# The second block's second mixer: a new order for its projections, its stick-breaking groups and its memory attention

## The reference, cut to the stage in question

```python
h = rms_norm_2(x, norm_pre_mix[1])
proj = h @ w_in_b[0]                 # 256 tokens x 1024 -> 2560
q, k, v = three parts of 768, as 12 heads of 64
mem_q = proj[..., 2304:]             # 256 wide, 4 heads of 64
# stick-breaking attention, for each block of 128 queries and all keys up to its end
z = q @ k.T / 8
before = s_idx < t_idx
log_1m_beta = where(before, log_sigmoid(-z), 0)
tail = cumsum(log_1m_beta, reversed) - log_1m_beta
mix = where(before, exp(log_sigmoid(z) + tail), 0) @ v
# memory attention over 256 memory tokens, whose keys and values were made early on
cross = softmax(mem_q @ mem_k.T / 8) @ mem_v
y = concatenate([mix, cross]) @ w_out[1]
```

## Time and profile before

| what | value |
|---|---|
| runs | 2134.07 us median of 3 (2133.82 to 2136.89) |
| profiled execution | 2134.89 us, of which the span is 2132.7 us |
| mean granted TensorE clock | 0.979 |
| busy in the span | PE 2046.2 us (96%), DVE 1528.1 (72%), ACT 1247.1 (58%), POOL 21.6 (1%) |
| the chain that ended last | PE 85%, DVE 7%, ACT 4%, issue 3%, SP's queue 1% |
| HBM | 447.62 MB read, 210 GB/s over the span |

### The profile page before, as it was taken

The page is one execution under the profiler, slowest core; times in us unless marked ns, Lnnn a source line. Parts: engine busy times, 40 slices in busy tenths (PEclk is TensorE's granted clock), DMA queues, the critical chain, the costliest instruction groups (busy, mean ns, idle before and its releaser), DMA issues.

```text
span 2132.7 us, 31892 instructions
## 1 busy us (share of the span) xinstructions
PE 2046.2 (96%) x12731; PEld 1834.2 (86%) x12731; DVE 1528.1 (72%) x1741; ACT 1247.1 (58%) x1458; POOL 21.6 (1%) x52
## 2 busy tenths in 40 slices
PE   8989999988999999999999999899999999989998
PEld 8978998988787888888888888799999998878997
DVE  7866777575889888888888888676746556456554
ACT  5674434554767777676767777546255445655443
POOL 2000000000000000000000000000000000000000
PEclk9999999999999999999999999799999999999999
DMA  7314555432789898989898989333014554414552
GB/s 245 116 43 138 180 200 191 152 108 80 281 309 379 313 384 308 382 309 374 317 372 320 373 320 335 119 119 119 21 60 158 186 184 132 150 40 149 194 181 100
DMA packets 263790, 450.12 MB, mean 211 GB/s; under 512 B 10401, under 2 KB 147082, under 8 KB 263690
## 3 DMA queue, kind: packets, MB, share of 16 engines
q1 hardware_dynamic: 263304, 448.37, 60.0%
q10 hardware_dynamic: 386, 0.32, 0.0%
HBM read 447.62 MB, written 1.05 MB: 210 GB/s over the span
## 4 chain that ended last, share of the span: by engine, by line
PE 85%; DVE 7%; ACT 4%; issue 3%; SPq 1%; DMA 0%; ACTq 0%; DVEq 0%
PE bank L2329 23%; PE bank L2331 22%; PE bank L2330 22%; PE bank L2502 3%; PE bank L2455 2%; PE bank L2504 2%; DVE w_lo L1497 1%; DVE w_lo L1902 1%; ACT w_hi L918 1%; PE bank L2704 1%; PE bank L2861 1%; PE bank L2357 1%; PE bank L2426 1%; ACT w_hi L1201 1%; PE bank L2558 1%
## 5 line engine op out<-in xcount | busy, mean ns | idle before, releaser
L1497 DVE TENSOR_TENSOR w_lo<-ring,w_hi 128x2048 fp32r<-128x2048 f32 x160 | 365.4, 2291 | 205.5 <-ACT w_hi L918 205.2
L2329 PE MATMUL bank<-w_hi,a_both 128*128 128x512 f32 (+1 forms) x1040 | 372.6, 358 | 11.4 <-DVE a_both L1932 4.2
L2329 PE MATMUL bank<-a_both,w_hi 128*128 128x256 f32 x1248 | 359.5, 288 | 12.7 <-DVE a_both L1529 4.7
L918 ACT ACTIVATE w_hi<-ring 128x2048 fp32r<-128x2048 f32 x160 | 304.6, 1908 | 107.2 <-PE bank L2331 100.6
L2331 PE MATMUL bank<-w_hi,a_both 128*128 128x512 f32 (+1 forms) x1040 | 364.4, 350 | 0.0
L2330 PE MATMUL bank<-w_lo,a_both 128*128 128x512 f32 (+1 forms) x1040 | 363.9, 350 | 0.0
L1902 DVE TENSOR_TENSOR w_lo<-ring,w_hi 128x2048 fp32r<-128x2048 f32 x144 | 326.9, 2288 | 51.1 <-ACT w_hi L1201 51.1
L2330 PE MATMUL bank<-a_both,w_hi 128*128 128x256 f32 x1248 | 355.8, 285 | 0.0
L2331 PE MATMUL bank<-a_both,w_lo 128*128 128x256 f32 x1248 | 355.6, 285 | 0.0
L1201 ACT ACTIVATE w_hi<-ring 128x2048 fp32r<-128x2048 f32 x144 | 275.7, 1919 | 90.1 <-PE bank L2331 89.4
L1902 DVE TENSOR_TENSOR w_lo<-work,w_hi 128x2048 fp32r<-128x2048 f32 x120 | 274.7, 2289 | 19.2 <-ACT w_hi L1201 17.0
(11 more groups left out here) (440 smaller groups left out, 2855.4 us busy)
## 6 DMA issues: line engine op xcount, KB each, us to landing
ring<-in_moe_w_up SPq DMA_DIRECT2D x72, 1024.0 KB, 6.5
work<-in_moe_w_gate SPq DMA_DIRECT2D x72, 1024.0 KB, 7.2
ring<-in_moe_w_down SPq DMA_DIRECT2D x56, 1024.0 KB, 6.3
work<-in_moe_w_down SPq DMA_DIRECT2D x32, 1024.0 KB, 6.4
ring<-in_w_up SPq DMA_DIRECT2D x32, 1024.0 KB, 5.3
ring<-in_w_down SPq DMA_DIRECT2D x32, 1024.0 KB, 4.9
ring<-in_moe_w_gate SPq DMA_DIRECT2D x16, 1024.0 KB, 5.1
work<-in_moe_w_up SPq DMA_DIRECT2D x16, 1024.0 KB, 7.7
```

Source lines behind the costliest of these rows:

```text
L918: return eng.activation(w_hi[:, slot, :], ring[:, slot, :], ACT.Copy)
L1497: V.tensor_tensor(w_lo[:, i % SLOTS, :], ring[:, i % SLOTS, :], w_hi[:, i % SLOTS, :].bitcast(F32), ALU.subtract).then_inc(lo_made, 1)
L2329: PE.matmul(out, left[0], right[0], start=start, stop=False, **kw)
```

## The change

It reorders the stage and splits tiles into halves; the same matmuls are made. On TensorE:

- The tile of memory queries comes first (`T_MQ1`), with the norm's sums.
- Queries and keys follow by halves, `query_key(i)`, i = 0 to 11; the tiles alternate between queries and keys, so that tile 2k and 2k+1 give head pairs 2k and 2k+1. Scores of group g are made as soon as its pairs are there.
- Memory steps 0 to 12, score groups 0 to 3, sums and outputs stand between the halves of queries, keys and values, in an order written out by hand. The banks' numbers are given out in the same order.
- The first tile of the second output projection goes by chunks of the input, in the order 0, 1, 2, 6, 7, 3, 4, 5 (6 and 7 are the memory heads), each when its heads are there, instead of waiting for all.

On ScalarE, the softplus of a group, its exponential, value copies, high parts and memory steps follow in the matching order. The memory heads are copied out of their bank to `mem_heads` (in `h`) when a pair is done, and split from there later. On VectorE, the four scalings of memory queries come first; the rest is interleaved too. `feed_lo` of output tiles 1 and 2 stands behind the heads 0 and 1 and the memory heads and ahead of heads 2 to 5.

The diff, cut to its core:

```diff
+        Y1_ORDER = (0, 1, 2, 6, 7, 3, 4, 5)
+        mem_heads = h[:, 0:2, :]
...
         A_DN0 = lend(4)
+        A_O3 = lend(2)
         A_SB = lend(6)
-        A_O3 = lend(2)
         A_DN1 = lend(4)
-        H_O1, H_O2, H_SB, H_O3 = 0, 8, 10, 16
+        H_O1, H_O2 = 0, 8
+        H_O3, H_SB = (10, 14), (11, 12, 13, 15, 16, 17)
...
-        T_INB = stream(*[C(a["w_in_b_2"][0], t, U_INB_QK + 2 * t + 2) for t in range(6)])
-        stream(*[C(a["w_in_b_2"][0], 6 + t, V_USES[t] + 2) for t in range(3)])
-        stream((*column_tile(a["w_in_b_2"][0], 3 * SW), "done", U_MQ1 + 2))
+        T_MQ1 = stream((*column_tile(a["w_in_b_2"][0], 3 * SW), "done", U_MQ1 + 2))
+        T_QK = stream(*[C(a["w_in_b_2"][0], t // 2 + 3 * (t % 2), U_QK[2 * t + 1] + 1) for t in range(6)])
+        T_SV = stream(*[C(a["w_in_b_2"][0], 6 + t, V_USES[2 * t + 1] + 1) for t in range(3)])
```

ScalarE's new order (helpers: `scores_out` three copies, `scores_soft` the softplus, `stick_weights` the exponential):

```diff
+            feed(T_MQ1 + SLOTS)
+            feed(T_QK + 0 + SLOTS)
+            memory_step(0)
+            feed(T_QK + 1 + SLOTS)
+            scores_out(0)
+            scores_soft(0)
+            memory_step(1)
+            memory_step(2)
+            feed(T_QK + 2 + SLOTS)
+            memory_step(3)
+            feed(T_QK + 3 + SLOTS)
+            memory_step(4)
+            scores_out(1)
+            scores_soft(1)
+            memory_step(5)
+            feed(T_QK + 4 + SLOTS)
+            stick_weights(0)
+            memory_step(6)
+            memory_step(7)
+            feed(T_QK + 5 + SLOTS)
+            scores_out(2)
             got(eng, U_RC)
+            value(0)
+            memory_step(8)
+            scores_soft(2)
+            value(1)
+            feed(T_SV + 0 + SLOTS)
+            memory_step(9)
+            stick_weights(1)
+            scores_out(3)
+            memory_heads(0)
+            value(2)
+            memory_step(10)
+            scores_soft(3)
+            value(3)
+            feed(T_SV + 1 + SLOTS)
+            stick_weights(2)
+            value(4)
+            memory_heads(1)
+            value(5)
+            for c in range(2):
+                split_heads(A_SB + c, H_SB[c], c)
+            stick_weights(3)
+            for c in range(2):
+                got_lent(eng, A_O3 + c)
+                eng.activation(a_hi[:, LH + c, :], mem_heads[:, c, :], ACT.Copy).then_inc(in_hi, 1)
+            split_heads(A_SB + 2, H_SB[2], 2)
+            feed(T_SV + 2 + SLOTS)
+            for c in range(3, SH // 2):
+                split_heads(A_SB + c, H_SB[c], c)
```

VectorE's (`query_key` scales one half, `soft_masked` is softplus and mask, `stick_logs` subtraction and mask):

```diff
+            eng.wait_ge(done, U_MQ1 + 2)
+            for k in range(2):
+                for half in range(2):
+                    rows_of = slice(64 * half, 64 * half + 64)
+                    ins = V.scalar_tensor_tensor(mq_pad[half][rows_of, k, :], bank(U_MQ1 + k)[rows_of, 0:T], 64 ** -0.5,
+                                                 rstd[rows_of, :], ALU.mult, ALU.mult)
+                give(ins, U_MQ1 + k)
+            feed_lo(T_MQ1 + SLOTS)
...
+            query_key(0)
+            query_key(1)
...
+            feed_lo(T_QK + 0 + SLOTS)
+            query_key(2)
+            query_key(3)
+            memory_max(0)
+            feed_lo(T_QK + 1 + SLOTS)
+            memory_scale(0)
+            query_key(4)
+            memory_max(1)
+            query_key(5)
+            memory_max(2)
+            soft_masked(0)
+            memory_scale(1)
+            memory_scale(2)
+            query_key(6)
+            memory_max(3)
+            feed_lo(T_QK + 2 + SLOTS)
+            query_key(7)
+            memory_scale(3)
+            memory_max(4)
+            feed_lo(T_QK + 3 + SLOTS)
+            memory_scale(4)
+            query_key(8)
+            stick_logs(0)
+            query_key(9)
+            memory_max(5)
+            memory_scale(5)
+            soft_masked(1)
+            query_key(10)
+            memory_max(6)
+            feed_lo(T_QK + 4 + SLOTS)
+            memory_scale(6)
+            query_key(11)
+            memory_max(7)
+            memory_scale(7)
+            feed_lo(T_QK + 5 + SLOTS)
+            stick_logs(1)
+            soft_masked(2)
+            feed_lo(T_SV + 0 + SLOTS)
+            stick_logs(2)
+            soft_masked(3)
+            stick_logs(3)
+            for c in range(2):
                 heads_lo(A_SB + c, I_Y1, c)
+            for c in range(2):
+                eng.wait_ge(in_hi, I_Y1 + 2 + c + 1)
+                V.tensor_tensor(a_lo[:, LH + c, :], mem_heads[:, c, :], a_hi[:, LH + c, :].bitcast(F32), ALU.subtract)
+            feed_lo(T_SV + 2 + SLOTS)
+            for c in range(2, SH // 2):
+                heads_lo(A_SB + c, I_Y1 + 2, c)
```

TensorE's:

```diff
+            project(T_MQ1, U_MQ1, R_B, sums=U_N_B)
+            query_key(0)
+            query_key(1)
             eng.wait_ge(rows_made, 1)
...
+            query_key(2)
+            query_key(3)
             got(eng, U_MQ1 + 1)
+            memory_step(0)
+            got(eng, U_QK[3])
+            stick_scores(0)
+            query_key(4)
+            memory_step(1)
+            query_key(5)
+            memory_step(2)
+            query_key(6)
+            memory_step(3)
+            query_key(7)
+            memory_step(4)
+            got(eng, U_QK[5])
+            got(eng, U_QK[7])
+            stick_scores(1)
+            query_key(8)
+            stick_sums(0)
+            query_key(9)
+            memory_step(5)
+            query_key(10)
+            memory_step(6)
+            query_key(11)
+            memory_step(7)
+            got(eng, U_QK[9])
+            got(eng, U_QK[11])
+            stick_scores(2)
+            value(0)
+            memory_step(8)
+            value(1)
+            stick_sums(1)
+            got(eng, V_USES[1])
+            stick_outputs(0)
+            memory_step(9)
+            stick_scores(3)
+            value(2)
+            memory_step(10)
+            value(3)
+            stick_sums(2)
+            got(eng, V_USES[3])
+            stick_outputs(1)
+            memory_step(11)
+            value(4)
+            memory_step(12)
+            stick_sums(3)
+            value(5)
+            got(eng, V_USES[5])
+            stick_outputs(2)
+            stick_outputs(3)
+            second_ffn(1, T_Y1, U_Y1, U_YS1, U_N_M1, T_UP1, U_UP1, U_RC1, A_DN1)
```

More of the change, by code:

```diff
@@ L413, in build, with memory_unit @@
         U_N_B = turn(1)
-        U_INB_QK = turn(12)
-        U_RC = turn(1)
[L417 to L427, removed]
+        U_MQ1 = turn(2)
+        U_QK, SBZ, SBR, V_USES = {}, {}, {}, {}
+        AT3 = {}, {}
+        def memory_unit(i):
+            if i < 2 * XH:
+                AT3[0][i] = turn(1)
+            if LAG <= i < 2 * XH + LAG:
+                AT3[1][i - LAG] = turn(1)
+        U_QK[0], U_QK[1] = turn(1), turn(1)
+        U_RC = turn(1)
+        U_QK[2], U_QK[3] = turn(1), turn(1)
+        memory_unit(0)
+        SBZ[0] = turn(SG)
+        U_QK[4] = turn(1)
+        memory_unit(1)
+        U_QK[5] = turn(1)
+        memory_unit(2)
+        U_QK[6] = turn(1)
+        memory_unit(3)
+        U_QK[7] = turn(1)
+        memory_unit(4)
+        SBZ[1] = turn(SG)
+        U_QK[8] = turn(1)
+        SBR[0] = turn(SG)
+        U_QK[9] = turn(1)
+        memory_unit(5)
+        U_QK[10] = turn(1)
+        memory_unit(6)
+        U_QK[11] = turn(1)
+        memory_unit(7)
+        SBZ[2] = turn(SG)
+        V_USES[0] = turn(1)
+        memory_unit(8)
+        V_USES[1] = turn(1)
+        SBR[1] = turn(SG)
+        memory_unit(9)
+        SBZ[3] = turn(SG)
+        V_USES[2] = turn(1)
+        memory_unit(10)
+        V_USES[3] = turn(1)
+        SBR[2] = turn(SG)
+        V_USES[4] = turn(1)
+        SBR[3] = turn(SG)
+        V_USES[5] = turn(1)
         U_Y1 = turn(8)
@@ L1425, in _ @@
             roots(U_N_B, ACT.Exp)
[L1426 to L1429, removed]
-            got(eng, U_RC)
[L1432 to L1462, removed]
@@ L1463, in _, with value, scores_out @@
-            for c in range(SH // 2):
-                split_heads(A_SB + c, H_SB + c, c)
-            attend(AT3, 2 * XH, False, 2 * NH + 2 * XH, A_O3, H_O3, LH)
+            def value(k):
+                n = V_USES[k]
+                t, j = k // 2, k % 2
+                eng.wait_ge(done, n + 1)
+                give(eng.activation(sv[:, j, 256 * t:256 * t + 256], bank(n)[:, 0:T], ACT.Copy,
+                                    scale=rstd_col[:, j:j + 1]), n)
+            def scores_out(g):
+                if g >= 2:
+                    eng.wait_ge(stick_a, g - 1)
+                for i in range(SG):
+                    n = SBZ[g] + i
+                    eng.wait_ge(done, n + 1)
+                    give(eng.activation(z_sb[:, g % 2, 3 * P * i:3 * P * i + 3 * P], bank(n)[:, 0:3 * P], ACT.Copy), n)
@@ L3044, in _, with query_key, value, memory_step @@
             scaled_tokens(U_DS0, y_tok, y_scale)
[L3047 to L3054 removed]
+            project(T_MQ1, U_MQ1, R_B, sums=U_N_B)
+            def query_key(i):
+                project_half(T_QK + i // 2, U_QK[i], i % 2)
```

(14 more changed lines are left out.)

138 lines of the change are left out of this document (67 added, 71 removed).

## The result

The changed kernel takes 2119.94 us (median of 4 runs, 2117.59 to 2121.23) against 2134.44 us of the kernel before: a ratio of 0.9929, 95% interval 0.9917 to 0.9941, 14.5 us less. Forecast were 2120.5 us and 13.6 less. The total was right; two of its terms were not, and their errors partly cancelled.

The account below looks back on a forecast made before the run. Matmul engine taken as bound by its own work, waits on three-engine chains and half-clock stretches. 122.7 against 105.8 us gave 16.9 less; minus 3.3 for clock, 13.6; 2134.07 - 13.6 = 2120.5 us, range 2114.5 to 2127.5.

Parts of the forecast that it names:

- The price list and the walk: In the reordered stretch: block prices sum to 99.9 us; carrying instructions engine by engine adds 5.9, giving 105.8 against 122.7.
- The three small waits: Matmul engine waits: 0.85 and 0.45 us at the second group's scores, 0.55 for the copy of value 5.
- The wait before chunk 2: Second output projection: chunk 2 waits 3.1 us, its low part queued on VectorE behind two weight tiles' low parts.
- 16.9 us less at full clock: Stage start to end of the output projection's first tile: 105.8 us against 122.7, before any charge for half clock.
- The clock: In the reordered stretch: two half-clock stretches charged, 3.3 us in all; none and four (6.6 us) were the ends.
- the pair of 0.85 and 0.45: Second group's scores: these two waits were taken to bring one half-clock stretch, as two waits of 0.8 us had.
- The rest "as before": From the second output tile on: same tiles, banks and due times, low parts ready earlier than wanted, so no change.
- The rule on table loads: ScalarE: a drain of 1.38 us beside each load, 2.66 per switch; value copies over 1 us late, about 2126 us.
- ScalarE late: Rival: each group's softplus 1.4 us late on ScalarE pushes the matmul engine four times, 5.6 us, to 2126; chance 0.18.
- Half clock throughout: Rival: clock stays at its lower level from 1808 on in the interleaved stretch, adding 70 us, to 2187; chance 0.04.
- Covers hold and the clock stays: Rival: only the 3.1 us wait, or VectorE ahead of the walk; 17 to 19 us less, 2115 to 2117; chance 0.13.
- A wait on a bank or a count as long as before: Rival: such a wait in the second group or before the output projection; within 4 us of now; chance 0.03.

Follow-up runs that it names:

- values late: Changed kernel with ScalarE's copies of values 1 and 3 moved behind a weight's high part; 2122.51 us.
- heads first: Changed kernel with VectorE making the low parts of heads 2 to 5 before those of output tiles 1 and 2; 2114.95 us.
- queries scaled early: Kernel before, with the memory queries' four scalings moved ahead of the fourth group's softplus on VectorE; 2133.68 us.

## Why the prediction was right

**The price list and the walk.** I forecast the end of the last outputs 96.8 us behind the stage's start; it came after 96.3. The three small waits were forecast at 0.85, 0.45 and 0.55 and came at 0.34, 0.59 and 0.56, the wait before the third tile was 0.1, not 0.2, and there was none before outputs 3 instead of 0.45. The wait before chunk 2 was forecast at 3.1 and was 2.7. The step that each tile's transfer lands in time held: no wait for a tile's transfer stands in the list. The second output tile started at 1899.98, inside the 1898 to 1902 that was named as a sign. So the term "16.9 us less at full clock" would have been 17.6: the stage's 16.1 and the 1.5 that its half-clock stretch cost.

**The clock.** This term was mis-sized: I charged two stretches, 3.3 us; there was one in the stage, 1.5 us, and it came where I had put it, behind the 2.7 us. The step that failed is "the pair of 0.85 and 0.45 resembles the two of 0.8": 0.34 and 0.59 had none, and 1.57 and 1.51 in the run with values late had none either. The reading behind it, one stretch behind each wait of 2.5 us and more and none behind 1.8, was that of one profile, and the second profile of the same kernel has an exception to either half. The stretch charged behind chunk 2 came in all three profiles with that wait of 2.7 (the changed kernel twice, values late). The prediction also puts the half clock of the kernel before at 16.6 us, with 6.1 for the third stretch; it is 17.0 and 6.8, and that stretch begins 0.7 us before its wait ends, so it does not stand wholly behind it. The stage was then 16.1 shorter, and not 13.6: of the 2.5 between, 1.8 are the clock's and 0.7 the walk's. In the walk itself two errors met. From the stage's start to the second output tile are 106.6 us; without 1.5 for the clock and 4.3 of waits, the matmul work is 100.8, where I had 99.9, and the waits were 5.9.

**The rest "as before".** This step was wrong: 1.2 us came back there. Both profiles show it, and the two errors, 2.5 and 1.2 us, are of opposite sign: that the total came within 1 us is in part luck. With the start of the stage 0.8 later in the profiled execution, the span is 14.1 shorter.

**The rule on table loads.** The Trainium skill (ScalarE: Activation LUTs, What ACT_TABLE_LOAD costs) has a drain beside each load. The changed kernel has its eight loads too, and on ScalarE's timeline the load at 1864.32 lasts 1.28 and the exponential starts at 1865.62. By that rule the value copies had come too late; they did not.

**The rivals.** ScalarE late: not so in the changed kernel, and with values late its mechanism was made and had about the price given. Half clock throughout: the 96.3 us up to the last outputs ran at 1.00. Covers hold and the clock stays: not so here, a stretch followed the chunk 2 wait both times; heads first, without that wait, had none in the stage and took 2114.95. A wait on a bank or a count as long as before: none is in the list.

## What to carry to other kernels

When chains over three engines need cover, try first to cut the bound engine's dense work into halves and to order them by what the chains wait for; here that, with the output projection by chunks, gave 17.9 us, more than the whole change, and the memory steps between the halves some 3 us more once the rest was right. In a hand-written order look at what each long, unhurried instruction stands in front of: two weight tiles' low parts, 4.5 us, ahead of a head's 0.4 cost 4.4 us in the stage in one place, clock included, and 5.4 ahead of a memory maximum in another. Fixing one wait of such a chain can be worth little (1.4 of 3.8 us at most); make the walk to the end before you believe it.

## What the runs showed of the hardware

Of the 16 waits of 2.5 us and more in the stages of the thirteen profiles (2.5 to 5.3), 15 have a stretch at 1.2 GHz behind or across their end, 3.4 or 6.8 us long; one of 2.5, in the second profile of the kernel before, has none. That of 1.8 before the output projection has one in two of three profiles (the second of the kernel before, and queries scaled early). The two of 0.8 to 1.0 us with 2 us of short matmuls between them have one behind them in all four profiles of the order before; single waits of 1.1 to 1.6 us in the stage have none. But 1.6 us was followed by one behind the stage in the changed kernel, twice, and by none at the same place in five other profiles. So the length of the wait alone does not decide, and neither does the kernel. A half-clock stretch of 3.4 us costs 1.5 us in dense matmuls, and nothing to 0.9 where it lies in a wait or ahead of one that takes it up.
